# A three-part transformer step on one core: the modulation vectors computed by matmuls with moving weight rows instead of by VectorE multiply-accumulate

## The reference, cut to what matters

```python
silu_c = jax.nn.silu(c)
silu_cc = jax.nn.silu(c_ctx)
m = jnp.split(silu_c @ w_ada[l] + b_ada[l], 6, axis=-1)      # w_ada[l]: 1024 x 6144
sh1, sc1, g1, sh2, sc2, g2 = [t[:, None, :] for t in m]
h = modulate(rms_norm(lat, g_norm1[l]), sh1, sc1)            # h * (1 + scale) + shift
```

## Time and profile before

| | us |
|---|---|
| three runs | 3319.67, 3322.84, 3329.49 |
| median | 3322.84 |
| profiled execution, span from first to last instruction | 3312.0 |
| busy in it: PE, PEld, DVE, ACT | 3079.7, 1744.9, 1093.9, 513.0 |
| of DVE, lines L1104 and L1106 (modulation) | 334.5 in L1104 alone |
| moved from memory | 685.91 MB, 207 GB/s over the span |

### The profile page before, as it was taken

One profiled execution on the slowest core, in us unless ns is written; L12 is line 12 of the kernel. 1 busy time (PEld: TensorE's weight loads), 2 busy tenths in 40 slices (PEclk: granted clock), 3 DMA queues, 4 the chain that ended last, 5 costly groups with the idle time before them and its releaser, 6 DMA issues.

```text
span 3312.0 us, 31972 instructions
## 1 busy us (share of the span) xinstructions
PE 3079.7 (93%) x12504; PEld 1744.9 (53%) x12504; DVE 1093.9 (33%) x2435; ACT 513.0 (15%) x1022; POOL 0.2 (0%) x4
## 2 busy tenths in 40 slices
PE   4898999998889999979978999899999899899998
PEld 3565444447754444434534444344444355487886
DVE  8653212228631222240436433353221213513002
ACT  1032111111021111120414000010000013301000
POOL 0000000000000000000000000000000000000000
PEclk8898999999889999989999999999999999899999
DMA  7627999997669999921010332133331131133440
GB/s 328 249 117 296 425 428 428 428 429 297 250 250 426 424 429 428 429 109 67 26 51 26 152 152 102 51 127 152 152 152 77 51 127 51 51 130 127 150 153 13
DMA packets 49552, 688.31 MB, mean 208 GB/s; under 512 B 5296, under 2 KB 7344, under 8 KB 7728
## 3 DMA queue, kind: packets, MB, share of 16 engines
q1 hardware_dynamic: 47696, 680.55, 50.1%
q10 hardware_dynamic: 1760, 6.43, 0.5%
HBM read 685.91 MB, written 1.05 MB: 207 GB/s over the span
## 4 chain that ended last, share of the span: by engine, by line
PE 87%; DVE 9%; issue 2%; ACT 1%; DMA 0%; ACTq 0%; DVEq 0%
PE bank L361 58%; PE bank L547 23%; DVE work L1104 4%; PE bank L405 2%; PE bank L432 1%; PE bank L423 1%; DVE X L1216 1%; DVE work L1005 1%; DVE MX L1066 1%; DVE work L1084 0%; PE bank L572 0%; DVE work L1106 0%; ACT work L806 0%; DMA par_sb<-in_par 0%; PE bank L589 0%
## 5 line engine op out<-in xcount | busy, mean ns | idle before, releaser
L361 PE MATMUL bank<-A,ring 128*128 128x256 f32 (+1 forms) x3088 | 1007.2, 487 | 23.4 <-issue 13.3
L361 PEld LDWEIGHTS bank<-A,ring 128*128 128x128 f32 x3088 | 598.9, 195 | 405.1 <-issue 342.4
L547 PE MATMUL bank<-ring,work 128*64 128x512 f32 x3072 | 673.3, 594 | 2.7 <-ACT work L891 2.7
L361 PE MATMUL bank<-work,ring 128*128 128x256 f32 (+1 forms) x1696 | 539.7, 476 | 12.5 <-DVE work L1012 8.2
L361 PEld LDWEIGHTS bank<-work,ring 128*128 128x128 f32 x1696 | 325.4, 192 | 216.4 <-issue 174.5
L547 PEld LDWEIGHTS bank<-ring,work 128*64 128x64 f32 x3072 | 216.7, 137 | 412.3 <-issue 408.4
L1104 DVE SCALAR_TENSOR_TENSOR work<-ring,SILC,work 128x512 f32<-128x512 f32 x476 | 334.5, 747 | 7.0
L361 PE MATMUL bank<-work 128*128 128x128 f32 (+3 forms) x2016 | 256.1, 304 | 15.6 <-DVE work L1205 8.7
L361 PEld LDWEIGHTS bank<-work 128*128 128x128 f32 (+2 forms) x2016 | 192.1, 174 | 39.9 <-issue 33.4
L1228 DVE TENSOR_TENSOR work<-work,bank 128x512 f32<-128x512 f32 x32 | 22.0, 688 | 380.2 <-PE bank L547 380.2
L1445 DVE TENSOR_TENSOR work<-work,bank 128x512 f32<-128x512 f32 (+1 forms) x44 | 24.4, 554 | 355.3 <-PE bank L361 355.3
(11 more groups left out here) (177 smaller groups left out, 1548.6 us busy)
## 6 DMA issues: line engine op xcount, KB each, us to landing
ring<-in_stream SPq DMA_DIRECT2D x324, 2048.0 KB, 12.1
X<-in_xt ACTq DMA_DIRECT2D x1, 2048.0 KB, 18.3
tab_sb<-in_tab_a ACTq DMA_DIRECT2D x1, 1120.0 KB, 25.4
X<-in_ctx2t ACTq DMA_DIRECT2D x1, 1024.0 KB, 7.3
out<-X SPq DMA_DIRECT2D x1, 1024.0 KB, 4.8
tab_sb<-in_tab_b ACTq DMA_DIRECT2D x1, 960.0 KB, 4.8
par_sb<-in_par ACTq DMA_DIRECT2D x1, 617.0 KB, 8.9
work<-in_wsp ACTq DMA_DIRECT2D x1, 512.0 KB, 31.1
```

The source lines that it names most:

```text
L361: m = pe.matmul(o, w, x, start=start, stop=stop)
L547: m = pe.matmul(o, w, x, start=start, stop=stop)
```

## The change

VectorE no longer multiplies. The silu values stand in `SILC` as 32 columns for each k, of which the first two are the two conditions and 30 are zero. `mod_rows(n)` on TensorE takes these 32 columns as stationary operand and the strip's 512 columns of piece k as moving one, and gives piece k to column group k % 4 of the array (`tile_position=(0, 32 * (k % 4))`), so that the pieces k and k + 4 sum up in one quarter of the partitions of `bank[4 + n % 2]`. VectorE copies that bank once (`mod_copy`), and `mod_columns(n)` sums the four quarters and turns the row into columns: four matmuls, with 128 x 128 of the copy as stationary operand and the 0/1 matrix `cond` (one column per condition) moving. For two conditions this is now four matmuls, where it was eight.

```diff
-        SILC = sb("SILC", [P, 2, KD, 2])
+        SILC = sb("SILC", [P, 2, KD, 32])
...
-            def reduce_mod(n):
+            def mod_rows(n):
+
+                st, which, _, _ = MODS[n]
+                W = strip(st)
+                if n >= 2:
+                    pe.wait_ge(mod_copied, n - 1)
+                for k in range(KD):
+                    q = 32 * (k % 4)
+                    m = mm(bank[4 + n % 2][q:q + 32, :], SILC[:, which // 2, k, :], W[:, k * 512:(k + 1) * 512],
+                           k < 4, k >= 4, tells=k == KD - 1, place=(0, q))
+                m.then_inc(mod_raw, 1)
+                used()
+
+            def mod_columns(n):
 
                 _, which, first, conds = MODS[n]
-                pe.wait_ge(mod_summed, n + 1)
-                used()
+                pe.wait_ge(mod_copied, n + 1)
                 for j in range(4):
                     col = (which * NMOD + first + j) * 2
-                    for s in range(conds):
-                        m = mm(bank[7][:, col + s:col + s + 1], macc(n, s)[:, j * P:(j + 1) * P], ones[:, 0:1],
-                               True, True, tells=j == 3 and s == conds - 1)
+                    m = mm(bank[7][:, col:col + conds], mrow(n)[:, j * P:(j + 1) * P], par_("cond", 0, conds),
+                           True, True, tells=j == 3)
                 m.then_inc(mod_done, 1)
...
-            pe.wait_ge(x_in, 16)
-            for n in range(2):
-                reduce_mod(n)
+            pe.wait_ge(silc_ready, 1)
+            for n in range(3):
+                mod_rows(n)
+                if n:
+                    mod_columns(n - 1)
             norm("n1_0", 2 * T)
-            for n in range(2, 4):
-                reduce_mod(n)
+            mod_rows(3)
+            mod_columns(2)
+            mod_columns(3)
...
                 if j == 1:
                     used()
-                    for n in range(7, 10):
-                        reduce_mod(n)
+                    mod_rows(7)
+                    mod_rows(8)
+                    mod_columns(7)
+                    mod_rows(9)
+                    mod_columns(8)
+                if j == 2:
+                    mod_columns(9)
...
-            for n in range(EVEN_OUT_MOD, ODD_MOD):
-                reduce_mod(n)
+            mod_rows(EVEN_OUT_MOD)
+            mod_rows(EVEN_OUT_MOD + 1)
+            norm("n2_0", T)
+            mod_columns(EVEN_OUT_MOD)
+            mod_rows(EVEN_OUT_MOD + 2)
+            mod_columns(EVEN_OUT_MOD + 1)
+            mod_columns(EVEN_OUT_MOD + 2)
...
+                    if l == 0 and j % 4 == 1 and j > 4:
+                        mod_columns(FFN_MOD + j // 4 - 1)
                     if j % 4 == 3:
                         used()
                         if l == 0:
-                            reduce_mod(FFN_MOD + j // 4)
+                            mod_rows(FFN_MOD + j // 4)
...
-            def mod_strip(n):
-
-                st, which, _, conds = MODS[n]
-                dve.wait_ge(strip_in[st % RING], 16 * (st // RING + 1))
...
-                            m = dve.scalar_tensor_tensor(macc(n, s), W, c, macc(n, s), ALU.mult, ALU.add)
...
+            def mod_copy(n):
+
+                dve.wait_ge(mod_raw, n + 1)
+                if n >= 2:
+                    dve.wait_ge(mod_done, n - 1)
+                dve.tensor_copy(mrow(n), bank[4 + n % 2][:, :]).then_inc(mod_copied, 1)
...
-            take_mods(0, 40, 48, 1, ODD_MOD)
-            take_mods(1, 0, 16, 1, ODD_MOD)
             link(gain(2, 0, 32, 0, par_("g2", 0, KD)))
             last_taken(dve, "even_out")
             norm("n2_0", T, lambda k: X[:, k, 0:T], lambda k: A[:, k, 0:T], [(0, T, lambda k: GSC[:, 2, k:k + 1])])
+            mod_copy(EVEN_OUT_MOD + 2)
+            take_mods(0, 40, 48, 1, ODD_MOD)
+            take_mods(1, 0, 16, 1, ODD_MOD)
             moe(0)
```

More of the change, by code:

```diff
@@ L77 @@
 MODS += [(s, 2, 16 + 4 * i, 2) for i, s in enumerate(places("l0_merge", "M"))]
+MERGE_AFTER = [(32 * (e + 1) - 1) // 12 for e in range(8)]
 FFN_MOD = len(MODS)
 MODS += [(s, 3, 4 * i, 2 if i < 4 else 1) for i, s in enumerate(places("l0_ffn", "M"))]
[L82 to L86, removed]
 LAYER_STREAMS = (2, 1)
@@ L148 @@
     ("gq", 4), ("gkv", 2), ("sink", HEADS), ("rbias", 2 * TB * ROUTES),
-    ("ident", P), ("ones", P), ("before", P), ("expert", EXPERTS), ("group", EXPERTS), ("slot", C),
+    ("ident", P), ("ones", P), ("before", P), ("expert", EXPERTS), ("group", EXPERTS), ("slot", C), ("cond", 2),
 ])
@@ L357, in tile, with mm @@
                 return v[:, at * P:(at + width) * P]
-            def mm(o, w, x, start, stop, tells=False):
-                m = pe.matmul(o, w, x, start=start, stop=stop)
+            def mm(o, w, x, start, stop, tells=False, place=None):
+                m = pe.matmul(o, w, x, start=start, stop=stop, tile_position=place)
                 if owed[0] and not tells:
@@ L462, in _ @@
             used()
-            for n in range(4, 7):
-                reduce_mod(n)
+            mod_rows(4)
+            mod_rows(5)
+            mod_columns(4)
+            mod_rows(6)
+            mod_columns(5)
             linear("even_k", 0, 2 * T, lambda k: tile("even", 32 + k), lambda k: A[:, k, :], KD)
+            mod_columns(6)
             b = group(GROUP0["even_v"])
@@ L486, in _ @@
             used()
-            for n in range(10, EVEN_OUT_MOD):
-                reduce_mod(n)
+            mod_rows(10)
+            mod_rows(11)
+            mod_columns(10)
+            mod_rows(12)
             used()
@@ L647, in _ @@
                        wait=normed("n1_1") if j == 0 else None)
+                if j >= 4 and j % 4 < len(range(*ODD_REDUCE[j // 4 - 1])):
+                    mod_columns(ODD_REDUCE[j // 4 - 1][0] + j % 4)
                 if j % 4 == 3:
@@ L1151, in _ @@
             for j in range(4):
-                if j < 3:
-                    mod_strip(4 + j)
                 dve.tensor_scalar(QRAW[:, j, :], take("even_q", j, T), 0.125, None, ALU.mult).then_inc(taken["D"], 1)
+            for n in range(4, 7):
+                mod_copy(n)
             dve.tensor_copy(QRAW[:, 4, :], take("even_k", 0)[:, 0:T])
@@ L1164, in _ @@
                 dve.tensor_tensor(o, QK[:, j, :], TMP1[:, j % 2, :], ALU.add).then_inc(rope_done, 1)
-            for n in range(7, EVEN_OUT_MOD):
-                mod_strip(n)
+            for n in range(7, 10):
+                mod_copy(n)
             for n in range(TB):
@@ L1171, in _ @@
                 dve.bn_aggr(BN[:, n, 6:8], BN[:, n, 0:6]).then_inc(z_var, 1)
+            mod_copy(10)
             for n in range(TB):
@@ L1176, in _ @@
                    .then_inc(z_norm, 1)
+            mod_copy(11)
+            mod_copy(12)
             dve.wait_ge(taken["A"], TAKEN[GROUP0["even_u"] + 3])
@@ L1323, in _ @@
             link(m)
[L1326 removed]
+            after_chunk = dict(zip((0, 1, 3, 4, 5, 7), ODD_REDUCE))
             for c in range(KD):
[L1328 to L1329 removed]
                 cw = lambda tap: par_("conv", tap * KD + c, 1)
@@ L1339, in _ @@
                 dve.tensor_tensor(CV[:, c, :], t_, BG[:, c % 2, :], ALU.mult).then_inc(cv_ready, 1)
+                for n in range(*after_chunk.get(c, (0, 0))):
+                    mod_copy(n)
             take_mods(1, 16, 48, 1, ODD_REDUCE[6][0])
@@ L1343, in _ @@
                 residual("odd_out", j, T, MOD[:, 1, 16 + j, 0:1])
-                if j in (0, 3):
-                    for n in range(*ODD_REDUCE[6 + j // 3]):
-                        mod_strip(n)
+                if j % 4 == 3:
+                    mod_copy(ODD_REDUCE[6 + j // 4][0])
             last_taken(dve, "odd_out")
@@ L1383, in outer @@
                         sum_up(j, w)
+                    if j in mod_after:
+                        mod_copy(mod_after[j])
             for l in range(2):
@@ L1435, in _ @@
                                .then_inc(taken["D"], 1)
+                        if l == 0 and o * 3 + b in MERGE_AFTER:
+                            mod_copy(MERGE_MOD + MERGE_AFTER.index(o * 3 + b))
                 if l == 0:
@@ L1446, in _ @@
                        .then_inc(taken["D"], 1)
-                if l == 0:
-                    mod_strip(FFN_MOD + 11)
-                outer(l, f"down{l}", 40, w)
+                    if l == 0 and j % 2:
+                        mod_copy(FFN_MOD + j // 2)
+                outer(l, f"down{l}", 40, w, {1: FFN_MOD + 11} if l == 0 else {})
                 if l == 0:
```

72 lines of the change are left out of this document (29 added, 43 removed).

## The result

| | before | after |
|---|---|---|
| median of 20 runs each, us | 3319.82 (3314.19 to 3329.49) | 3333.15 (3323.59 to 3348.66) |
| ratio, 95% interval | | 1.0043 (1.0031 to 1.0056) |
| profiled execution, span, us | 3312.0 | 3325.7 |
| PE, DVE busy, us | 3079.7, 1093.9 | 3134.2, 770.0 |

The change makes the kernel slower, by 0.43%. I had forecast no change (3322, range 3308 to 3348): the time lies inside the range, 11 us above the forecast. The kernel before has a median of 3319.82 over 20 runs, where I had 3322.84 from three, so the change is worth +13.3 us where my sum said -0.5.

The account below looks back on a forecast made before the run. The prediction took TensorE as the bound (87% of the chain), with 64.4 us of waits for VectorE's modulation sums against 76 us more TensorE work. Place-by-place terms summed to -0.5 us, giving 3322 us, range 3308 to 3348.

Parts of the forecast that it names:

- What one strip costs: TensorE's work per modulation strip: row matmuls R = 1.95 us, column sums C = 0.85 us, together 2.8.
- Start: Kernel start, strips 0 to 3: landings bound it, vectors taken at 45.4 us instead of 54.2; -8.8, bounds -11 and -5.
- Even mixer: Strips 4 to 12: fewer waits and less slow clock behind them, against more matmuls; -8.3 us together.
- Attention: Stretch from 160 to 212 us: new column sums fill part of the pause ahead; -3 us, between 0 and -7.
- Behind `even_out`: Norm and routing behind the even mixer: routing 5.3 us later, as it also waits for `take_mods`; +5 us.
- Merge: Eight strips in the merge: 22.4 us after the change for 28.3 before; -5.9 us.
- Odd mixer: Modulation in 760 to 906 us: 35.6 us for 33.7, less 1.4 for a faster norm behind; +0.5 us.
- Feed-forward: Twelve strips with no wait to remove: 33.6 us for 13.6; +20 us, the largest term.
- pairs: Rival for the strips' row matmuls: only two column groups run at once, R = 3.7; +80 us, 3402; chance 0.12.
- Four share something: Rival for the strips' row matmuls: four groups slow each other, R = 2.5; +26 us, 3348; chance 0.15.
- The clock: Rival: TensorE waits less, so attention, start norm and routing run at a higher clock; -9 us more, 3313; chance 0.13.
- The copies: Rival: column sums wait for VectorE's late `mod_copy` in more places than the one counted; +8 us, 3330; chance 0.08.

Follow-up runs that it names:

- e5: The changed kernel with executed filler on TensorE, 10 one-element matmuls at the start and 46 ahead of the second expert part; 3320.37 us, ratio 0.9994.
- e2: The changed kernel without the overflow branch on TensorE (flag load, jump and the code jumped over); 3318.67 us, ratio 0.9996 to the kernel before.
- e6: The kernel before the change, with 16 one-element matmuls added at its start on TensorE; 3333.66 us, ratio 1.0031.
- e10: The changed kernel with two column groups instead of four for a strip's pieces; 3410.85 us, ratio 1.0254 to the kernel before.
- e3: The changed kernel with a strip's eight pieces issued in the order 0, 4, 1, 5, 2, 6, 3, 7; 3328.03 us, ratio 1.0021 to the kernel before.
- e11: The changed kernel with only 10 executed one-element filler matmuls on TensorE at the start; 3326.17 us, ratio 1.0006 to the kernel before.
- e1: The changed kernel with 32 never-executed matmuls written into the overflow branch behind the first expert loop; 3330.73 us, ratio 1.0033 to the kernel before.

## Why the prediction was wrong, point by point

- **What one strip costs: right.** R 1.85 for 1.95, C 0.81 for 0.85. The four groups ran as the two of the earlier trace rows do. The rule from the Trainium skill, page "TensorE: Matmul & The Clock Gate", section "Part 3: Packing small matmuls" (2.38 for three column tiles, 3.07 for four row tiles; 3346 here), did not hold for this shape: one group takes 6.98 and four 1.85, a factor of 3.8 with the change of form included.
- **Start: right in mechanism, 2 too small** (-10.9 for -8.8): the landings bound it, and the norm ran partly at full clock.
- **Even mixer: right** (-8.9 from the start of `even_q` to attention's first matmul, 99.0 before and 90.1 after, for -8.3).
- **Attention: the -3 did not come** in the profiled execution: 53.5 us from its first matmul to `even_out`, before (159.02 to 212.50) and after (139.17 to 192.65). This term was a guess between 0 and -7, and the stretch changes by itself from one execution to the next, as told below.
- **Behind `even_out`: right** (+5.6 for +5). **Merge: right** (-5.5 for -5.9, by e5, which has no stall in that row). **Odd mixer: right** (0 for +0.5, once the slow norm at its head is counted with the exit). **Feed-forward: right** (+20.9 from norm to norm for +20). PE's busy time rose by 54.5 us and not by the some 70 that I had named as a sign.
- **The step that failed** is the sentence "The sum must be made place by place": the places were those with modulation work, and the two exits of the expert loops were none. They were so put at nothing, and cost +4.2 (a wait of 5.82 for 1.60) and +2.0 (the norm behind it ran at a granted clock of 0.60 where it had 1.00, 6.71 for 4.72) at the first, and +4.2 at the second (from the norm's first record to the end of its last 8.9 us for 4.7), together 10.4; the table, against e2 and e5, has 9.0 and 9.4. The measured span is 14.2 above my sum: 10.4 here, 3 for attention, 0.8 between the routing of `moe0` and the first matmul of its loop (25.8 us for 25.0), and the rest cancels. It is a cost of where the code lies, whatever that code computes: e6 has it without the change, and e5 has the change without it.
- **The rivals**: pairs priced right and absent (e10). "Four share something" (3348) had the right sign, which is luck: its reason is excluded by R = 1.85. The clock did not pay in the profiled execution, since attention kept its slow start (granted clock 0.53 in 159.0 to 176.4 before, 0.54 in 139.2 to 156.4 after). The copies were waited for 3.9 us in all, as counted.
- Without the fetches the forecast of no change would have held: e2 and e5 have ratios of 0.9996 and 0.9994. The medians make the loss larger than the rows do: from e2 to the changed kernel 0.0047, 16 us, for 9 to 10. e3, with the same two waits as the changed kernel, stands at 1.0021. What makes two sets of 10 to 20 runs differ by so much was not found.

## What to carry to other kernels

Cost a change stage by stage, also where nothing stands ahead of it to remove: this one was worth -25 us in three stages (start, even mixer, merge) and cost 6 and 21 in two others, and leaving it out of the feed-forward, where VectorE was not waited for, turned a loss of 0.43% into a gain of 0.34%. A kernel with a branch or a loop has a fourth resource beside engines, memory and queues: where its code lies. When a wait for "issue" appears at the first instructions behind a jump, look for the instruction queue's transfers in the 3 us ahead of where the engine goes on, and test by shifting the code with filler in an idle place before believing any other story; a difference of 0.3% between two versions may be nothing else. In such a kernel an A/B test of a small change needs its time with the code shifted, on both sides.

## What the runs showed of the hardware that I had not expected

- **A jump of some 450 instructions costs TensorE either nothing or 4 us**, by where it stands. With the 1.6 us for the squares the wait is 5.5 to 6.3 us where the instructions behind the jump have to be waited for, 1.6 to 2.3 where they are there or nearly so, and in the third picture the norm begins on time and stops for 2.6 to 3.4 behind its first three or four records. All 28 exits of the 14 profiled executions fit one of these three. The norm behind the full wait runs slower, 2 us in most (6.4 to 6.8 for 4.7; 5.9 in e11).
- **The loop itself fetched nothing.** In 300 to 735 after the change, some 14 of the 16 turns of a body of 78 matmuls (over 300 instructions), the transfers show of the instruction queues this one packet of q14, and none of q8:

```profile
q14 instruction: 1, 0.01, 0.0%
```

  The second loop (960 to 1405) shows one packet of q8, and so do the first of e6 and both of the kernel before: never one for every turn. So code that has been run stays at hand when the jump goes back; it is the forward jump that misses. The Trainium skill, page "Runtime: NRT & Kernel Launch", section "Instruction fetch mechanics", gives TensorE 128 KiB for its instructions in one sentence and two blocks of 16 KiB in another. A body of over 300 instructions lies in two blocks or in three, and its place isn't known, so no run here decides between the two.
- **Executions of the same code differ by up to 17 us ahead of the first routing** (first row of the table: after, e1, e2 and e11 are the same there but for 10 tiny matmuls in e11, and show 237.1, 236.9, 253.8, 236.5). Part of it is how long attention stays at the lower of the two clocks. In the changed kernel's execution the granted clock is 0.54 in 139.2 to 156.4 and 1.00 from 160 on; in e3's, with the same matmuls there, it is 0.50 in 152 to 176 and 1.00 only from 179.6 on. First the changed kernel, then e3:

```profile
152.38 2.07 PE L353 MATMUL bank<-work 64*128 64x512 f32 x2
...
160.05 1.12 PE L353 MATMUL bank<-work 64*128 64x512 f32 x2
```

```profile
172.07 2.07 PE L353 MATMUL bank<-work 64*128 64x512 f32 x2
...
179.59 1.12 PE L353 MATMUL bank<-work 64*128 64x512 f32 x2
```

  The same matmuls take 2.07 and 1.12, and attention 53.5 and 63.1 us. One profiled execution is therefore good for durations and for stages, and no evidence on 10 us of the total; for that, the medians of 10 and more runs are better. What decides when the clock rises was not tried.
